# Second mixer, sparse branch: the two heads of a pair turned in the step of the next pair's scores

## The reference

```python
z = h @ w_in                                   # split into the inputs of three branches
o_nsa = nsa_attention(...)                     # 8 heads of 64, sparse
o_gla = gated_linear_attention(...)            # 4 heads
o_mem = memory_attention(...)                  # 4 heads
merged = (gates[:, :, 0] * (o_nsa @ w_branch[0]) + gates[:, :, 1] * (o_gla @ w_branch[1])
          + gates[:, :, 2] * (o_mem @ w_branch[2]))
x = x + merged @ w_out
```

```python
return gb[..., 0:1] * o_c + gb[..., 1:2] * o_s + gb[..., 2:3] * o_w
```

## Time and profile before

| | |
|---|---|
| median of 3 runs | 1879.52 us |
| profiled execution | 1880.13 us, its span 1878.7 us |
| PE busy | 1872.5 us, 100% |
| DVE, ACT busy | 1033.4 and 1035.0 us, 55% each |
| POOL busy | 1555.6 us, 83% |
| granted TensorE clock | 1.000 |
| second mixer's sparse steps | 1077 to 1194 us and 1531 to 1649 us |

### The profile page before, as it was taken

How to read it: one execution, slowest core, us unless ns; L and a number is a source line. 1 busy time by engine, 2 the same in 40 slices (tenths; PEclk the granted TensorE clock), 3 DMA queues, 4 the chain that set the end, 5 groups by cost and what they waited for, 6 DMA issues and landing times.

```text
span 1878.7 us, 27088 instructions
## 1 busy us (share of the span) xinstructions
PE 1872.5 (100%) x9604; PEld 1549.8 (82%) x9604; DVE 1033.4 (55%) x2654; ACT 1035.0 (55%) x1765; POOL 1555.6 (83%) x1102
## 2 busy tenths in 40 slices
PE   9999999999999999999999999999999999999999
PEld 8888887888888889788888877888888877788887
DVE  5338565434676756554344677446444477645542
ACT  7445666444744576654466454665456554566543
POOL 8988886988798878698879787779887968778986
DMA  7665444565565553367556343456657533345553
GB/s 285 243 231 182 166 135 157 192 198 192 204 236 196 190 169 135 132 220 261 196 187 255 124 146 117 154 184 220 235 191 260 169 126 133 124 165 194 192 197 138
DMA packets 98419, 348.94 MB, mean 186 GB/s; under 512 B 13260, under 2 KB 13932, under 8 KB 97772
## 3 DMA queue, kind: packets, MB, share of 16 engines
q1 hardware_dynamic: 97708, 346.06, 54.0%
q10 hardware_dynamic: 576, 1.14, 0.2%
HBM read 346.11 MB, written 1.05 MB: 185 GB/s over the span
## 4 chain that ended last, share of the span: by engine, by line
PE 99%; DVE 1%; ACT 0%; issue 0%; ACTq 0%
PE psum L661 28%; PE psum L663 28%; PE psum L662 28%; PE psum L689 1%; PE psum L691 1%; PE psum L692 1%; PE psum L945 1%; PE psum L759 1%; PE psum L935 1%; PE psum L958 1%; PE psum L1204 1%; PE psum L925 0%; PE psum L1361 0%; PE psum L1155 0%; PE psum L832 0%; PE psum L828 0%
## 5 line engine op out<-in xcount | busy, mean ns | idle before, releaser
L634 POOL TENSOR_TENSOR lo<-raw,hi 128x256 fp32r<-128x256 f32 (+2 forms) x1070 | 1520.4, 1443 | 298.3 <-ACT hi L1509 270.4
L1509 ACT ACTIVATE hi<-raw 128x1024 fp32r<-128x1024 f32 (+1 forms) x613 | 639.1, 1052 | 495.7 <-PE psum L663 461.6
L661 PE MATMUL psum<-hi,h_hi 128*128 128x512 f32 (+1 forms) x1504 | 592.6, 394 | 0.0
L663 PE MATMUL psum<-hi,h_lo 128*128 128x512 f32 (+1 forms) x1504 | 583.6, 388 | 0.0
L662 PE MATMUL psum<-lo,h_hi 128*128 128x512 f32 (+1 forms) x1504 | 583.0, 388 | 0.0
L2211 DVE STREAM_TRANSPOSE psum<-big 32x128 f32<-32x128 f32 (+1 forms) x960 | 344.0, 358 | 14.2
L661 PEld LDWEIGHTS psum<-hi,h_hi 128*128 128x128 f32 x1504 | 282.5, 188 | 59.0 <-issue 2.1
L663 PEld LDWEIGHTS psum<-hi,h_lo 128*128 128x128 f32 x1504 | 282.3, 188 | 58.9
L661 PE MATMUL psum<-hi,y_hi 128*128 128x512 f32 x832 | 328.1, 394 | 0.0
L662 PEld LDWEIGHTS psum<-lo,h_hi 128*128 128x128 f32 x1504 | 282.7, 188 | 54.8
L663 PE MATMUL psum<-hi,y_lo 128*128 128x512 f32 x832 | 324.3, 390 | 0.0
(11 more groups left out here) (355 smaller groups left out, 1599.4 us busy)
## 6 DMA issues: line engine op xcount, KB each, us to landing
raw<-in_stream SPq DMA_DIRECT2D x607, 512.0 KB, 3.4
big<-in_w SPq DMA_DIRECT2D x14, 512.0 KB, 7.1
big<-in_post SPq DMA_DIRECT2D x6, 512.0 KB, 4.7
special<-in_b_merge SPq DMA_DIRECT2D x2, 1536.0 KB, 7.4
raw<-in_stream SPq DMA_DIRECT2D x8, 296.0 KB, 5.6
memkv<-in_mem_turned SPq DMA_DIRECT2D x2, 1024.0 KB, 6.9
big<-in_band SPq DMA_DIRECT2D x2, 768.0 KB, 4.9
raw<-in_first SPq DMA_DIRECT2D x2, 512.0 KB, 4.1
```

The source lines that it names most:

```text
L634: t = pool.tensor_tensor(M.lo[:, slot, w], M.raw[:, slot, w], f32(M.hi[:, slot_hi, w]), ALU.subtract)
L661: pe.matmul(out, lhs_hi, rhs_hi, start=start, stop=False)
L663: return pe.matmul(out, lhs_lo, rhs_hi, start=False, stop=stop)
L1509: act.activation(M.hi[:, slot_hi, used], M.raw[:, slot, used], ACT.Copy).then_inc(sem["hi"], 1)
```

## The change

The steps are drawn up anew. `nsa_pair` k multiplies the values of pair k-2, computes the scores of pair k and turns both heads of pair k-1: the first into bank 6 as before, the second into the idle bank of the strip (for the last pair, whose turn has no scores beside it, into bank 4). `nsa_norm` k, in a list behind a later piece, has DVE normalise both heads. The number of places in which small work stands between pieces falls from 23 to 15 a layer. The core of the diff (the new functions of ACT follow the same order):

```diff
--- before.py
+++ after.py
@@ -136,7 +137,9 @@
     mu = [("mem_unit", t) for t in range(6)]
     gu = [[("gla_unit", hp, m) for m in range(MT + 1)] for hp in range(2)]
     decay = [[("decay", hp, i) for i in range(4)] for hp in range(2)]
-    nu = [("nsa_unit", t) for t in range(NSA_UNITS + 2)]
+    cmp_unit = ("nsa_unit", 0)
+    pair = [("nsa_pair", k) for k in range(NSA_PAIRS + PAIRS_AHEAD + 1)]
+    norm = [("nsa_norm", k) for k in range(NSA_PAIRS)]
     none = ()
     return {
         "nk": (none, none, none, none),
@@ -147,14 +150,14 @@
         "mv": ([mem[8], mem[5]], cmp[4:8] + [mem[6]], [("take_cmp",), mem[7]], [mu[0]]),
         "gqk": ([mu[1]], [nsa[0], mu[2]], [mu[3], nsa[1]], [nsa[6], nsa[2]]),
         "gv": ([nsa[7], mu[4], nsa[3]], [gla[0]], [mu[5], nsa[4]], [gla[1], nsa[5]]),
-        ("merge", 0): ([gla[2], nu[0]], [decay[0][0]], [nu[1], decay[0][1]], none),
-        ("merge", 1): ([nu[2], decay[0][2]], [nu[3]], [decay[0][3]], [nu[4]]),
-        ("merge", 2): (none, [nu[5]], [gu[0][0]], [nu[6]]),
-        ("merge", 3): (none, [nu[7]], [gu[0][1]], [nu[8], decay[1][0]]),
-        ("merge", 4): ([gu[0][2], nu[9], decay[1][1]], [nu[10]], [nu[11], decay[1][2]], [nu[12], decay[1][3]]),
-        ("merge", 5): (none, [nu[13]], [gu[1][0]], [nu[14]]),
-        "gr": (none, [nu[15]], [gu[1][1]], [nu[16]]),
-        ("rows", 2): ([nu[17]], [nu[18], gu[1][2]], [gla[3]], [gla[4], gla[5]]),
+        ("merge", 0): ([gla[2], cmp_unit], [decay[0][0]], [pair[0], decay[0][1]], [norm[0]]),
+        ("merge", 1): ([decay[0][2]], [pair[1]], [norm[1], decay[0][3]], none),
+        ("merge", 2): ([pair[2]], [norm[2]], [gu[0][0]], none),
+        ("merge", 3): ([pair[3]], [norm[3]], [gu[0][1]], [decay[1][0]]),
+        ("merge", 4): ([gu[0][2], pair[4], decay[1][1]], [norm[4]], [pair[5], decay[1][2]], [norm[5], decay[1][3]]),
+        ("merge", 5): ([pair[6]], [norm[6]], [gu[1][0]], none),
+        "gr": ([pair[7]], [norm[7]], [gu[1][1]], none),
+        ("rows", 2): (none, [gu[1][2], pair[8]], [pair[9], gla[3]], [gla[4], gla[5]]),
         ("rows", 0): (none, [gla[6]], [gla[7]], none),
         ("rows", 1): (none, none),
     }
@@ -1309,16 +1313,41 @@
             j, b = (u - 1) // 4, (u - 1) // 2 % 2
             causal_scores(1, qT[:, j, :], kT[:, b, :])
 
-        def nsa_turn(u):
-            if u == 0:
-                pe.wait_ge(sem["cprob"], layer + 1)
-                wait_free("turned")
-                for m in range(MT):
-                    t = pe.transpose(psum[:, TURNED, m * P:m * P + P], V.pc[:, m * P:m * P + P], V.ident)
-                t.then_inc(sem["cturn"], 1)
-                free["turned"] = ("cpt", layer + 1)
-                return
-            turn_blocks(u % 2, BLOCKS)
+        def cmp_turn():
+            pe.wait_ge(sem["cprob"], layer + 1)
+            wait_free("turned")
+            for m in range(MT):
+                t = pe.transpose(psum[:, TURNED, m * P:m * P + P], V.pc[:, m * P:m * P + P], V.ident)
+            t.then_inc(sem["cturn"], 1)
+            free["turned"] = ("cpt", layer + 1)
+
+        def second_bank(k):
+            last = k + PAIRS_AHEAD >= NSA_PAIRS
+            return (0, SCORE[0]) if last else ("idle", idle_banks(strip_now)[0])
+
+        def turn_pair(k):
+
+            for slot in (1, 0):
+                prob = V.nsa_prob[k % PAIRS_AHEAD][slot]
+                pe.wait_ge(sem["prob"], nxt("prob"))
+                name, bank = ("turned", TURNED) if slot else second_bank(k)
+                if name == "idle":
+                    evicted(strip_now + 1)
+                wait_free(name)
+                for i, col in enumerate(BLOCKS):
+                    t = pe.transpose(psum[:, bank, i * P:i * P + P], prob[:, col:col + P], V.ident)
+                t.then_inc(sem["pturn"], 1)
+                free[name] = ("pt", nxt("taken"))
+
+        def nsa_pair(k):
+            if k > PAIRS_AHEAD:
+                nsa_outs(2 * (k - PAIRS_AHEAD) - 1)
+            if k < NSA_PAIRS:
+                nsa_score(2 * k + 1)
+            if k == 0:
+                cmp_turn()
+            if 0 <= k - PAIRS_AHEAD < NSA_PAIRS:
+                turn_pair(k - PAIRS_AHEAD)
 
         def nsa_outs(u):
             j, b = (u - 1) // 4, (u - 1) // 2 % 2
@@ -2240,19 +2264,22 @@
         dve.wait_ge(sem[name_hi], nxt(name_hi))
         dve.tensor_tensor(out, src, f32(high), ALU.subtract).then_inc(sem[name_lo], 1)
 
-    def minima(slot, tables, segments, scores=None):
-
-        prob, mn = soft[:, slot, 0, :], V.stat[slot][0]
+    def minima(slot, tables, segments, scores=None, prob=None, used=None):
+
+        prob, mn = soft[:, slot, 0, :] if prob is None else prob, V.stat[slot][0]
         if not scores:
             dve.wait_ge(sem["score"], nxt("score"))
-        wait_used(prob_used, slot)
+        if used:
+            dve.wait_ge(sem["pturn"], used)
+        else:
+            wait_used(prob_used, slot)
         for i, ((col, width), table) in enumerate(zip(segments, tables)):
             w = slice(col, col + width)
             dve.tensor_tensor_reduce(prob[:, w], scores[i] if scores else psum[:, SCORE[slot], w], table, 1.0, HUGE,
                                      ALU.add, ALU.min, mn[:, i:i + 1]).then_inc(sem["mn"], 1)
 
@@ -2683,32 +2710,34 @@
             dve.tensor_tensor(all3, all3, inv16.unsqueeze(2).broadcast_to((P, 16, 16)),
                               ALU.mult).then_inc(sem["cprob"], 1)
 
-        def nsa_unit(t):
-            if t == 0:
-                cmp_probs()
-            elif t % 2 and t < NSA_UNITS:
-                minima(1, (V.causal[:, P:S], V.causal), SEG)
-            if t % 2 == 0 and t >= 4:
+        def nsa_pair(k, strip):
+            done, turned = k - PAIRS_AHEAD - 1, k - PAIRS_AHEAD
+            if done >= 0:
                 for slot in (1, 0):
                     pt_used[slot] = ("o", nxt("o"))
-                if t % 4 == 2:
-                    j = (t - 3) // 4
-                    col = S * (j % 2)
-                    kt = Y2_TILE[0] + j
-                    low_part(y_lo[:, kt, :], psum[:, OUT, col:col + S], y_hi[:, kt, :], "y2hi", "y2lo")
-            if t == 1:
+            if k < NSA_PAIRS:
+                for slot in (1, 0):
+                    used = n["pturn"] + 2 - slot if turned >= 0 else None
+                    minima(slot, (V.causal[:, P:S], V.causal), SEG, prob=V.nsa_prob[k % PAIRS_AHEAD][slot], used=used)
+            if k == 0:
                 dve.wait_ge(sem["cturn"], layer + 1)
                 dve.tensor_copy(V.pct, psum[:, TURNED, 0:S]).then_inc(sem["cpt"], 1)
-            elif 1 <= t - 1 < NSA_UNITS:
-                take_turned((t - 1) % 2, 384)
-            if t % 2 and t < NSA_UNITS:
-                minima(0, (V.causal[:, P:S], V.causal), SEG)
-            if t == 0:
-                cmp_finish()
-            elif t < NSA_UNITS:
-                j, b, g = (t - 1) // 4, (t - 1) // 2 % 2, (t - 1) % 2
-                at = (1 + b) * 8 + 2 * j + g
-                normalise(t % 2, SEG, [V.gates[:, m, at:at + 1] for m in range(MT)])
+            if 0 <= turned < NSA_PAIRS:
+                take_turned(1, 384)
+                dve.wait_ge(sem["pturn"], nxt("pturn"))
+                prob_used[0] = ("pturn", n["pturn"])
+                wait_used(pt_used, 0)
+                bank = idle_banks(strip)[0] if k < NSA_PAIRS else SCORE[0]
+                dve.tensor_copy(soft[:, 0, 1, 0:384], psum[:, bank, 0:384]).then_inc(sem["pt"], 1)
+            if done >= 0 and done % 2:
+                j = done // 2
+                col, kt = S * (j % 2), Y2_TILE[0] + j
+                low_part(y_lo[:, kt, :], psum[:, OUT, col:col + S], y_hi[:, kt, :], "y2hi", "y2lo")
+
+        def nsa_norm(k):
+            for slot in (1, 0):
+                at = (1 + k % 2) * 8 + 2 * (k // 2) + 1 - slot
+                normalise(slot, SEG, [V.gates[:, m, at:at + 1] for m in range(MT)], V.nsa_prob[k % PAIRS_AHEAD][slot])
 
         def branch(b, m):
 
```

More of the change, by code:

```diff
@@ L67 @@
 BAND_SLOT = (3, 0, 1)
-NSA_UNITS = 17
+NSA_PAIRS = 8
+PAIRS_AHEAD = 1
 Y1_EVENT = {3: 1, 4: 1, 5: 2, 6: 3, 7: 4, 0: 5, 1: 6, 2: 7}
@@ L417, in __init__ @@
         self.merged = self.merge[:, :, 2 * D:3 * D]
+        self.nsa_prob = [[M.soft[:, slot, 0, 0:384] for slot in range(2)]]
         self.q_buf = M.memkv[:, :, :].rearrange("p m c -> p (m c)").rearrange("p (l t) -> p l t", l=8)
@@ L1409, in mix2 @@
             elif what == "nsa_unit":
-                t = step[1]
-                if t in (0, 1, 3):
-                    nsa_score(t)
-                if t % 2 == 0 and t >= 4:
[L1414 to L1418, removed]
+                nsa_score(0)
+            elif what == "nsa_pair":
+                nsa_pair(step[1])
             elif what == "rows":
@@ L1665, in turn_qk, with exponentials @@
                            scale=scale).then_inc(sem["qk"], 1)
-    def exponentials(slot, segments):
-        prob = soft[:, slot, 0, :]
+    def exponentials(slot, segments, prob=None):
```

(33 more changed lines are left out.)

6 lines of the change are left out of this document (2 added, 4 removed).

## The result

The changed kernel takes 1886.75 us (median of six runs, 1886.32 to 1888.05), the kernel before 1879.51 in the same comparison: **+7.24 us**, a ratio of 1.0039, 95% interval [1.0027, 1.0051]. The forecast was +3.5, with 1879.2 to 1887.5 as its range. The direction is as forecast and the time lies inside the range, but the size is twice the forecast, nearer to rival (b).

A forecast was written before the change was run, and what follows sets the result against it. PE, busy the whole span, was taken as the bound. New waits of 2.85 us a layer, 5.7 in both, less 2.2 saved gave +3.5: 1883.0 us from 1879.52, range 1879.2 to 1887.5.

The forecast's parts named there:

- rival (b): DVE stays contended: pair 6 waits 2.4 us, pair 2 0.8, strip "gr" 0.5; +8.6, 1888.1 us; chance 0.15.
- What the change takes off PE: Eight fewer switches a layer at 0.05 us each, plus one wait gone: 0.7 us a layer, together 1.1.
- The lost wait: Turn behind ("merge", 4) piece 0: PE's 0.61 us stand for DVE's bank copy L2581 goes.
- Rows of branch 2: Seventh product of ("rows", 2) piece 0 waits for ACT to finish "gr": 1.2 us a layer, bounds 1.0 and 1.4.
- Gate of branch 2: PE's next rows tile waits for the first quarter of L2722: 0.5 us a layer, bounds 0.2 and 1.0.
- Pair 6: PE waits at the second turn for DVE's queue to normalise both heads: 1.0 us a layer; slowest rows 2.4.
- Pair 2: Second turn waits for DVE to take strip ("merge", 1)'s bank, L2782: 0.15 us a layer, 0 to 1.0.
- (a): Pair 6 fits: PE waits neither there nor at pair 2; +1.2, 1880.7 us; chance 0.20.
- (c): Joined turns ride along free, each returning 0.37 us: -1.6, 1877.9 us, chance 0.06; with no new waits 1872 to 1877, 0.04.

The follow-up runs named there:

- e8_before_turn9: Kernel before the change, with the turn that waits for the copy L2581 (sparse step nu[9]) moved one piece later: 1880.01 us, +0.08.
- e4_all: Changed kernel with decay[0][3] and norm[7] later, decay[1][2] and gu[1][1] earlier, the last two sparse steps one piece earlier: 1878.52 us, 1.12 below the kernel before.

## Why the prediction was right in direction and wrong in size

- *What the change takes off PE*: forecast 1.1 a layer, measured 0.99. In the trace a turn joined to the step ahead adds 0.34 (pair 2's step takes 2.95 with both turns, 2.61 with one), and 0.37 alone: joining returns 0.03 a turn, where I had 0.05. The lost wait is the larger part, and e8_before_turn9 shows that moving the one turn alone keeps a wait of that size (0.74).
- *Rows of branch 2*: forecast 1.2, measured 1.25, behind L1885 as named.
- *Gate of branch 2*: forecast 0.5 (its terms add up to 1200.3, not 1200.4), measured 0.42; only e4_all takes its cause away, together with others.
- *Pair 6*: **mis-sized**, 1.0 against 1.78. The term that was off is "1.32 for each normalisation, the row nearest to them". They took 1.60 and 1.55, 0.5 more; the minima began 0.7 behind the first turn where I had 0.5, and PE came 0.1 earlier. The upper end, 2.4, held.
- *Pair 2*: **mis-sized**, 0.15 against 1.03, just over the end of 1.0. The term that was off is "One more normalisation, 1.28 there, now stands ahead". By the forecast's own numbers, a take done at 1105.7 and PE there at 1105.9, nothing was left to wait for; the 0.15 was an allowance. I added one normalisation to a queue and left the rows of its other work at their price of before. Here both normalisations took 1.64, 0.72 more in sum, and the decay products 3.34 for 2.81, 0.53 more. PE came when I said, allowing for the 0.65 us by which this run reached the mixer earlier.
- *Between forecast and rival (b)*: (b) set decay pairs over 3.3 and normalisations over 1.7 as its mark. Pair 2 has the first and nearly the second, pair 6 neither; strip "gr" was not late. The forecast's own band, 1881.5 to 1884.7, is missed; the range held because it took in most of (b). What speaks for (b) is the same fact that mis-sized both terms. A price read from a row where POOL paused, or where the instruction happened to begin first, as at 1100.26, is not the price inside a run of POOL, and POOL is busy 82% of the span. With the dear prices for every instruction in the run, pair 2 comes out at 1105.7 + 0.72 + 0.53 + 0.1 - 1105.9 = 1.15 and pair 6 at 1.0 + 0.5 = 1.5.
- *Rivals (a) and (c)*: (a) fell with the same prices. (c) is refuted by e4_all, which has no new wait left in its list and gains 1.1 us in all.

## What to carry to other kernels

Where the instructions of two engines slow each other down, read an instruction's price from rows inside a run of the other engine, and reprice the whole queue, not only the part that was added: a cheap row can be a matter of which of two began first. Joining small steps gained 0.03 us each here, but needs all of their inputs at once, so before joining, look at what stands between the inputs and the step on each queue, and move that first: here four small moves in a table were worth 8 us, and the joining itself 1 to 2, at the edge of what the runs can tell from nothing.

## What the runs showed of the hardware that I had not expected

The loss of a DVE instruction goes with the length of one POOL instruction and not with the bytes that POOL moves: beside the same low parts, cut in halves, quarters or eighths, a product loses 1.09, 0.54 or 0.27 us, and the kernels take +23.1 (some 5.5 of it PE's lower clock), +7.2 and +3.4 us. It is the length of POOL's instruction that can be chosen, against its own cost per instruction (0.51 us for 128 columns, 0.77 for 256, means beside DVE). Each instruction of a normalisation, which reads one tensor in place and two columns of scalars, loses nearly as much as the products with two tensors: means of 0.34 us alone and 0.72 to 0.79 in a run of POOL. Beside zeros, where a product loses nothing, it still reads up to 0.37. POOL pays as well: an instruction of 256 columns that a product had come ahead of took 1.74 us.
